# A hybrid decoder trunk: gate and up products of the FFN from seven blocks in place of eight, down projection in two rounds

## What is computed

```python
def rmsnorm(x, g):
    xf = x.astype(jnp.float32)
    y = xf * lax.rsqrt(jnp.mean(xf * xf, axis=-1, keepdims=True) + NORM_EPS)
    return (y * g.astype(jnp.float32)).astype(x.dtype)

def swiglu(h, w_gate, w_up, w_down):
    return (jax.nn.silu(h @ w_gate) * (h @ w_up)) @ w_down
...
        xp = xp + swiglu(rmsnorm(xp, norm_ffn[i]), ffn_w_gate[i], ffn_w_up[i], ffn_w_down[i])
        xs = xs + swiglu(rmsnorm(xs, norm_ffn[i]), ffn_w_gate[i], ffn_w_up[i], ffn_w_down[i])
```

## Time and profile before

| | |
|---|---|
| median of the runs | 2143.99 us (2139.22 to 2148.89, 3 runs) |
| the profiled execution | 2140.05 us |
| its span, first to last instruction | 2138.3 us |
| mean granted clock of TensorE | 0.996 of full |
| products of TensorE | 17508 |

### The profile page before, as it was taken

One profiled execution on the slowest core, in us unless ns is written; L12 is line 12 of the kernel. 1 busy time (PEld: TensorE's weight loads), 2 busy tenths in 40 slices (PEclk: granted clock), 3 DMA queues, 4 the chain that ended last, 5 costly groups with the idle time before them and its releaser, 6 DMA issues.

```text
span 2138.3 us, 42249 instructions
## 1 busy us (share of the span) xinstructions
PE 2095.1 (98%) x17508; PEld 2026.4 (95%) x17508; DVE 1004.1 (47%) x1374; ACT 912.0 (43%) x1218; POOL 263.6 (12%) x253
## 2 busy tenths in 40 slices
PE   8999999999899999999999979999999999999999
PEld 7999999997499999999999859999999989999999
DVE  6444433368764444333566646444442264444322
ACT  6434432265454344322677744434432263443221
POOL 4000001169320000001111122000001120000000
PEclk9999999999999999999999999999999999999999
DMA  5333333244223333332532433333323313333332
GB/s 186 94 93 93 88 91 92 67 126 118 58 80 89 93 93 88 91 92 78 174 119 81 141 126 99 89 88 89 98 84 89 110 51 94 97 88 89 96 103 59
DMA packets 349435, 207.24 MB, mean 97 GB/s; under 512 B 9385, under 2 KB 340041, under 8 KB 349300
## 3 DMA queue, kind: packets, MB, share of 16 engines
q1 hardware_dynamic: 345476, 198.26, 31.4%
q0 software_dynamic: 3472, 6.96, 1.0%
q10 hardware_dynamic: 384, 0.55, 0.1%
HBM read 194.53 MB, written 8.60 MB: 95 GB/s over the span
## 4 chain that ended last, share of the span: by engine, by line
PE 89%; POOL 4%; ACT 3%; DVE 3%; issue 1%; DMA 0%; SPq 0%; POOLq 0%; ACTq 0%; DVEq 0%
PE acc L564 82%; POOL conv L2149 4%; PE pair L929 1%; PE bank L949 1%; PE pair L904 1%; PE pair L645 1%; DVE pair L1776 1%; ACT w_hi L1160 1%; PE pair L1098 0%; ACT s_buf L1430 0%; DVE w_lo L1573 0%; PE bank L939 0%; PE acc L984 0%; PE acc L973 0%; PE acc L799 0%
## 5 line engine op out<-in xcount | busy, mean ns | idle before, releaser
L564 PE MATMUL acc<-xin_hi,w_hi 128*128 128x260 f32 x3456 | 982.5, 284 | 5.9 <-DVE w_lo L1573 4.7
L564 PE MATMUL acc<-xin_hi,w_lo 128*128 128x260 f32 x3456 | 976.5, 283 | 0.0
L564 PE MATMUL acc<-xin_lo,w_hi 128*128 128x260 f32 x3456 | 973.6, 282 | 0.0
L1160 ACT ACTIVATE w_hi<-raw 128x1024 fp32r<-128x1024 f32 (+1 forms) x332 | 344.9, 1039 | 972.8 <-PE acc L564 970.0
L564 PEld LDWEIGHTS acc<-xin_hi,w_hi 128*128 128x128 f32 x3456 | 650.4, 188 | 20.4 <-issue 13.9
L564 PEld LDWEIGHTS acc<-xin_lo,w_hi 128*128 128x128 f32 x3456 | 650.0, 188 | 0.2
L564 PEld LDWEIGHTS acc<-xin_hi,w_lo 128*128 128x128 f32 x3456 | 650.1, 188 | 0.0
L1573 DVE TENSOR_TENSOR w_lo<-raw,w_hi 128x1024 fp32r<-128x1024 f32 (+1 forms) x332 | 411.0, 1238 | 350.2 <-ACT w_hi L1160 350.1
L564 PE MATMUL acc<-h_hi,w_hi 128*128 128x260 f32 x1408 | 398.4, 283 | 0.0
L564 PE MATMUL acc<-h_lo,w_hi 128*128 128x260 f32 x1408 | 398.2, 283 | 0.0
L564 PE MATMUL acc<-h_hi,w_lo 128*128 128x260 f32 x1408 | 397.6, 282 | 0.0
(11 more groups left out here) (356 smaller groups left out, 1846.5 us busy)
## 6 DMA issues: line engine op xcount, KB each, us to landing
raw<-in_ffn_w_gate SPq DMA_DIRECT2D x88, 512.0 KB, 3.9
raw<-in_ffn_w_up SPq DMA_DIRECT2D x88, 512.0 KB, 3.9
raw<-in_ffn_w_down SPq DMA_DIRECT2D x64, 512.0 KB, 4.0
raw<-in_ffn_w_down SPq DMA_DIRECT2D x32, 384.0 KB, 3.5
raw<-in_attn_w_qkv SPq DMA_DIRECT2D x24, 512.0 KB, 3.9
raw<-in_conv_w_in SPq DMA_DIRECT2D x16, 512.0 KB, 4.0
raw<-in_conv_w_out SPq DMA_DIRECT2D x8, 512.0 KB, 4.3
in_mix<-in_cache_k SPq DMA_DIRECT2D x8, 512.0 KB, 5.0
```

What stands on the lines that cost most here:

```text
L564: last = pe.matmul(acc[:, b, 0:HALF], w[:, w_tile * P:(w_tile + 1) * P], v[:, h * HALF:(h + 1) * HALF], start=start and t == 0, stop=stop ...
L1160: act.activation(w_hi[n.slot(2)][:, 0:cols], raw[:, n.slot(4), 0:cols], ACT.Copy).then_inc(split_hi, 1)
```

## The change

Of the 22 pairs of a layer, four stay as they were ("plain", PLAIN = 4). For the other 18 the sum over the 1024 input channels is cut in two halves of 512, and the 520 tokens in two halves of 260. Gate and up tile are the two rows, the halves of the input channels the inner dimension, the halves of the tokens the columns of a product of 2x2 blocks. It is made from seven block products (of 4 weight tiles, 3 terms each) in place of eight, with sums and differences of blocks before and after:

- GpSimd makes four sums of weight blocks for each pair (w_sum, 512 columns each); it waits for both loads, and for low splits of the pair before (`sums`: behind that pair's fifth split for the first three, behind its last for the fourth).
- x is multiplied by gain and rstd once (xn0, xn1 by VectorE, 16 operations of 260 columns), GpSimd makes four differences of 1040 columns (xt, xt3), ScalarE and VectorE split seven blocks of x of 1040 columns (`x_high`, `x_low`).
- Weight blocks are split by the block, 512 columns, into a ring of seven (w_hi, w_lo and ring_hi, ring_lo); `high` and `low` of the next pair stand between the steps that `join` this one.
- Seven banks take one block each. ScalarE copies the first out; VectorE makes five sums from the banks, 260 or 520 columns each (`join`), then h2 = up2*silu2 and h_lo. The silu is made in halves of 260 columns, without a multiplication by rstd.
- TensorE waits before a pair's first block for the fourth of the five sums of the pair before (joined), which frees the two banks of pair.
- h_hi and h_lo hold 11 tiles, not 22. So a layer is: 4 plain and 7 block pairs, the down products of these 11 tiles (8 output tiles, units of 6 and 5 weight tiles), 11 block pairs, the down products of those. x is updated in both rounds. SyncE, ScalarE and VectorE follow this order.

The core of the diff. The buffers, banks and names of semaphores are left out, and the parts that only carry the new names of units.

```diff
+PLAIN = 4
+ROUND = (PLAIN + 7, 11)
+FH = 11
+PAIRS = FT - PLAIN
+FIRST_PAIR = (0, ROUND[0] - PLAIN)
...
+        X_SUMMED = (0, 0, 2, 4, 1, 3, 0)
+        X_READ = (1, 3, 3, 4, 2, 3, 0)
+        BLOCK_BANK = tuple(acc[:, b, 0:HALF] for b in (0, 2, 1, 3)) + (pair[:, 1, 0:HALF], pair[:, 0, 0:HALF], bank6[:, 0:HALF])
+        W_SUM = (None, None, 1, 2, 0, None, 3)
...
+                for half in range(2):
+                    first_j, last_j = FIRST_PAIR[half], (FIRST_PAIR[1], PAIRS)[half]
+                    for j in range(first_j, last_j):
+                        for g in range(2):
+                            if j < first_j + 2:
+                                sp.wait_ge(split_lo, base + DOWN[half] - 4 + 2 * (j - first_j) + g + 1)
+                            else:
+                                sp.wait_ge(blk_lo, 7 * (PAIRS * layer + j - 1))
+                            into_raw((raw_of_pair(layer, j) + g) % 4, gate_up(g, PLAIN + j), 1024)
...
+                def block(J, b, x_from):
+                    pe.wait_ge(blk_lo, (J.times(7) + (b + 1)).v)
+                    if x_from:
+                        pe.wait_ge(xs_lo_ok, 7 * layer + b + 1)
+                    to = BLOCK_BANK[b]
+                    hi, lo = ring(w_hi, ring_hi, b), ring(w_lo, ring_lo, b)
+                    _, x_hi, x_lo = XS[b]
+                    for k in range(4):
+                        cols = slice(k * P, (k + 1) * P)
+                        for t, (w, v) in enumerate(((hi, x_hi), (hi, x_lo), (lo, x_hi))):
+                            last = pe.matmul(to, w[:, cols], v[:, k, :], start=k + t == 0, stop=k == 3 and t == 2)
+                    last.then_inc(blk_done, 1)
+                def seven_blocks(J, half=None):
+                    x_from = half == 0
+                    if half is not None:
+                        pe.wait_ge(evacuated, m0 + DOWN_M[half] - 1)
+                    if J.i is not None or J.start:
+                        pe.wait_ge(first_ok, J.v)
+                        pe.wait_ge(joined, (J.times(5) + -1).v)
+                    block(J, 0, x_from)
+                    if half is not None:
+                        pe.wait_ge(evacuated, m0 + DOWN_M[half])
+                    for b in range(1, 6):
+                        block(J, b, x_from)
+                    if J.i is not None or J.start:
+                        pe.wait_ge(joined, J.times(5).v)
+                    block(J, 6, x_from)
+                def down(half, i):
                     for c in range(4):
-                        m = at(m0 + 2 * FT + c, 4, i)
-                        for j, (k0, k1) in enumerate(((0, 8), (8, 16), (16, FT))):
+                        d, m = at(u + DOWN[half] + 2 * c, 8, i), at(m0 + DOWN_M[half] + c, 4, i)
+                        for j, (k0, k1) in enumerate(((0, 6), (6, FH))):
                             def before(k):
-                                pe.wait_ge(h_lo_ok, FT * layer + k + 1)
-                            unit(at(u + 2 * FT + 3 * c + j, 12, i), m, h_hi, h_lo, k0, k1, FT,
-                                 before if c == 0 else None)
-                            if layer >= 2 and j == 0 and i + c:
+                                pe.wait_ge(h_lo_ok, FT * layer + FH * half + k + 1)
+                            unit(d + j, m, h_hi, h_lo, k0, k1, FH, before if c == 0 else None)
...
+                def x_high(b):
+                    act.wait_ge(x_scaled, layer + 1)
+                    if X_SUMMED[b]:
+                        act.wait_ge(x_summed, 4 * layer + X_SUMMED[b])
+                    own, hi, _ = XS[b]
+                    act.activation(hi, own, ACT.Copy).then_inc(xs_hi_ok, 1)
...
+                def high(J, q, b):
+                    if b < 2:
+                        act.wait_ge(landed[q.slot(4)], (q.turn(4).v + 1) * 16)
+                    elif b == 5:
+                        act.wait_ge(landed[(q + 1).slot(4)], ((q + 1).turn(4).v + 1) * 16)
+                    else:
+                        act.wait_ge(w_summed, (J.times(4) + (W_SUM[b] + 1)).v)
+                    act.activation(ring(w_hi, ring_hi, b), block_of(b, q), ACT.Copy).then_inc(blk_hi, 1)
+                def join(p, fh, nxt):
+                    for b in range(7):
+                        act.wait_ge(blk_done, (p.times(7) + (b + 1)).v)
+                        if b == 0:
+                            act.activation(first[:], acc[:, 0, 0:HALF], ACT.Copy).then_inc(first_ok, 1)
+                        if b == 4:
+                            act.wait_ge(joined, (p.times(5) + 1).v)
+                            act.activation(silu2[:, 0:HALF], silu2[:, 0:HALF], ACT.Silu).then_inc(gate0_ok, 1)
+                        if b < 6:
+                            nxt(b)
+                    f = fh + FT * layer
+                    act.wait_ge(joined, (p.times(5) + 5).v)
+                    act.activation(silu2[:, HALF:T], silu2[:, HALF:T], ACT.Silu).then_inc(sg_ready, 1)
+                    nxt(6)
+                    act.wait_ge(h_ready, (f + 1).v)
+                    act.activation(tile_of(h_hi, fh + -FH * (fh.start >= FH)), h2[:], ACT.Copy).then_inc(h_hi_ok, 1)
...
+                    for b in range(7):
+                        act.wait_ge(units_done, units - (b < 2))
+                        high(At(J0), At(q0), b)
+                        if half == 0 and b in (3, 4):
+                            x_high(b + 2)
+                    with act.Fori(0, (count - 1) // 2) as i:
+                        for c in range(2):
+                            def nxt(b):
+                                high(At(J0 + 1 + c, 2, i), At(q0 + 2 + 2 * c, 4, i), b)
+                            join(At(J0 + c, 2, i), At(f0 + c, 2, i), nxt)
...
+                def scaled(k):
+                    g = vec[:, V_FFN + 8 * layer + k:V_FFN + 8 * layer + k + 1]
+                    for h, to in enumerate((xn0, xn1)):
+                        cols = slice(h * HALF, (h + 1) * HALF)
+                        last = dve.scalar_tensor_tensor(to[:, k, :], x[:, k, cols], g, rstd[:, cols], ALU.mult, ALU.mult)
+                    return last
...
+                    dve.tensor_tensor(h2[:], up2[:], silu2, ALU.mult).then_inc(h_ready, 1)
+                    if c + 1 < PLAIN:
                         split(n + 3)
-                        dve.wait_ge(h_hi_ok, (f + (FT * layer + 1)).v)
-                        dve.tensor_tensor(tile_of(h_lo, f), h_buf[:, c, :], tile_of(h_hi, f).bitcast(F32), ALU.subtract)\
-                           .then_inc(h_lo_ok, 1)
+                    dve.wait_ge(h_hi_ok, f + 1)
+                    dve.tensor_tensor(h_lo[:, c, :], h2[:], h_hi[:, c, :].bitcast(F32), ALU.subtract).then_inc(h_lo_ok, 1)
+                    if c == 0:
+                        for k in range(4, KT):
+                            last = scaled(k)
+                        last.then_inc(x_scaled, 1)
+                    for b in ((), (0,), (1, 2, 3), (4,))[c]:
+                        x_low(b)
...
+                def low(J, q, b):
+                    dve.wait_ge(blk_hi, (J.times(7) + (b + 1)).v)
+                    dve.tensor_tensor(ring(w_lo, ring_lo, b), block_of(b, q), ring(w_hi, ring_hi, b).bitcast(F32), ALU.subtract)\
+                       .then_inc(blk_lo, 1)
+                def join(p, fh, nxt):
+                    done, made = p.times(7), p.times(5)
+                    dve.wait_ge(blk_done, (done + 1).v)
+                    nxt(0)
+                    dve.wait_ge(blk_done, (done + 2).v)
+                    nxt(1)
+                    dve.wait_ge(blk_done, (done + 3).v)
+                    dve.wait_ge(first_ok, (p + 1).v)
+                    dve.tensor_tensor(begun[:, 0:2, :], acc[:, 1:3, 0:HALF], first[:].unsqueeze(1).to_broadcast([P, 2, HALF]), ALU.add)                       .then_inc(joined, 1)
+                    nxt(2)
+                    dve.wait_ge(blk_done, (done + 4).v)
+                    dve.wait_ge(joined, (made + 1).v)
+                    dve.tensor_tensor(with_t3[:], acc[:, 3, 0:HALF], with_t2, ALU.add).then_inc(joined, 1)
+                    nxt(3)
+                    dve.wait_ge(blk_done, (done + 5).v)
+                    dve.tensor_tensor(with_t1[:], BLOCK_BANK[4], with_t2, ALU.add).then_inc(joined, 1)
+                    nxt(4)
+                    dve.wait_ge(blk_done, (done + 6).v)
+                    dve.wait_ge(joined, (made + 2).v)
+                    dve.tensor_tensor(halves(up2[:]), pair[:, :, 0:HALF], with_t3[:].unsqueeze(1).to_broadcast([P, 2, HALF]), ALU.add)                       .then_inc(joined, 1)
+                    nxt(5)
+                    dve.wait_ge(blk_done, (done + 7).v)
+                    dve.wait_ge(joined, (made + 3).v)
+                    dve.tensor_tensor(silu2[:, HALF:T], BLOCK_BANK[6], with_t1[:], ALU.add).then_inc(joined, 1)
+                    f = fh + FT * layer
+                    dve.wait_ge(sg_ready, (f + 1).v)
+                    dve.wait_ge(joined, (made + 5).v)
```

(45 more changed lines are left out.)

308 lines of the change are left out of this document (218 added, 90 removed).

## The result

| | before | after |
|---|---|---|
| median of the runs, us | 2141.66 (2139.22 to 2148.89) | 2170.78 (2168.77 to 2175.86) |
| profiled execution, us (span) | 2140.05 (2138.3) | 2175.86 (2173.9) |
| TensorE busy, us (products) | 2095.1 (17508) | 2034.7 (16644) |

A forecast was written before the change was run, and what follows sets the result against it. TensorE bounds the old kernel; in the changed pair loops VectorE, held up by GpSimd's sums, would at 11.3 us a pair. 2140 + 22 (layers) + 2 (rest) = 2164; with the median 3.9 higher, 2168, range 2112 to 2208.

The forecast's parts named there:

- TensorE's share: Block pairs on TensorE: 84 products in place of 96, 10.06 us against 11.50; 103.5 us saved at most.
- rival A: Pair loops: TensorE stays the bound as GpSimd's sums miss VectorE's splits; pair 10.06 us, median 2077; chance 0.12.
- VectorE alone, 8.87 us: VectorE's operations and waits in a pair, without GpSimd's interference, sum to 8.87 us, less than TensorE's 10.06.
- The door: SBUF access shared by GpSimd and VectorE: an addition costs VectorE 1.0 us when its next instruction reads SBUF twice.
- The layout: Pair's instructions laid out from the fifth split's end: GpSimd's sums delay VectorE, giving a period of 11.3 us.
- The start of a round: TensorE waits 5.4 us before a layer's first block pair, 1.6 before the eighth; first bank release after 15.0 and 12.1.
- A layer: A layer's 18 block pairs gain 1.4 us and pay 7.0 for the starts: +5.6, +22 in four layers.
- Table loads: ScalarE's table loads, 11 a layer, should leave the pair loops; if they stay, its idle 4 us a pair hide them.
- Loads of weights: Both loads of a pair land 10.9 us after issue, just before GpSimd's sums need them; no cost counted.
- rival D: TensorE's pauses lower its clock to 1.2 GHz in places; 3.4 us at half pace eat 1.2; chance 0.19 with rival C.
- The sum: Whole kernel: 2140 + 22 + 2 = 2164 us for the profiled execution; median forecast 2168.
- rival C: Pair loops: GpSimd holds 1.30 us or late loads make three sums block fully; period 11.8 to 12.1; 0.19 with rival D.

The follow-up runs named there:

- the probe with 8 columns: Changed kernel with GpSimd's four sums a pair cut to 8 columns of constants, splits of those blocks taking raw weights: 2079.83 us, ratio 0.9691.
- second order: Changed kernel with splits and PSUM sums reordered, third PSUM sum behind the fifth split, GpSimd's fourth sum released by its pair's second split: 2127.89 us, ratio 0.9933.
- third order: Kernel of the second order with the sixth and seventh split moved behind h_lo, so five splits follow in a row: 2132.3 us, ratio 0.9949.

## Why the prediction was right, step by step

- **TensorE's share.** 10.06 us a pair and 103.5 us at most: the last pair of a round, which follows no backlog, came 9.8 after the one before it, and without GpSimd's holds the time was 2079.8 (rival A's 2077). That rival's mechanism was right and only its condition wasn't met.
- **VectorE alone, 8.87 us.** Its operations have the predicted prices (0.69, 0.42; 0.58 idle for the silu, of the 0.67 laid out); alone they are no bound, as the probe with 8 columns shows.
- **The door.** An addition was to cost 1.0 when the next operation reads SBUF twice; it cost 1.1 (1.78 for 0.69). By the Trainium skill (GPSIMD Engine Reference, Elementwise — side-by-side cycle accounting) an fp32 addition with two inputs goes at some 2.6 cycles an element at 1.2 GHz; 512 elements would be 1.11 us, an estimate that agrees with the hold better than the record of 1.27 does. The layout put the holds on the sixth split (0.6), the seventh and the next pair's first (1.07 each): the trace has 0.68, 1.1 and 1.1, in just these places. The period laid out was 11.3; it is 11.30 to 11.34 in 47 of the 56 pairs, 11.5 at the head of each second round, and 11.5 to 11.9 in five single pairs.
- **The start of a round.** 5.4 and 1.6 were predicted, 5.3 and 1.5 are there. The way from the first split to the first release, 15.0 and 12.1 in the forecast, is 14.4 to 14.7 and 12.4, but that is luck, as its parts don't hold: none of the seven splits was held in these first pairs. GpSimd's first sum was kept out instead (below), its third and fourth came late, and VectorE waited 2.6 us for the high half of a sum. Round one took 81.7 us from the end of its first split to the first down product, as predicted, round two 125.0 for 124.0.
- **A layer.** Forecast +5.6 and 0.5 for the rest; measured +8.1, +7.6, +7.0 and +8.2 by the spans above. Five late pairs and the four heads of second rounds, 2.8 us together, are 0.7 of the 1.6 that are missing in the mean layer; I haven't found the rest in one place.
- **Table loads** left the pair loops: four are left where the silu of the plain tiles starts. **Loads of weights** are in time in 51 of the 56 pairs; the other five stand behind this list.
- **The clock** (rival D) stays at 1.00 in the steady pairs with TensorE busy 91% of the time (47.17 of 51.90 us, 126.5 to 178.4), as expected. It falls to 0.50 once in each round. In the first rounds that is at the start, where TensorE is ahead, as the forecast had it. In the second rounds it is for 3.4 us behind the 2.3 us that TensorE waits for the first `up`; this makes the 11.5 at their head, 0.2 us each, as rival D has it for a fall in mid-round. Where it cost most, before layer 0, no step of mine had looked.
- **The sum**: +24 for the profiled execution; its layers took +30.8, so the mechanism was right and the terms a little small (6.1 a layer for 7.7). Medians moved +29.1 against +24; that the forecast's 2168 stands only 2.8 below the median is partly luck, as the median before is now 2141.66 and no longer the 2143.99 from which it was worked out.

In five pairs GpSimd's first sum began 0.2 to 1.2 us late. In four of them the profile puts it down to the load of the up tile; in the fifth it names a split that had long been done, so there too it was probably a load:

```profile
726.92 1.72 POOL L2445 TENSOR_TENSOR w_sum<-raw 128x512 f32<-128x512 f32 x1 [4.88 <-DMA raw<-in_ffn_w_up]
```

In four of the five the sixth split goes free and three full holds follow, on the seventh, h_lo and the next pair's first, and the period is 11.7 to 11.9. That is what rival C describes. The forecast let the loads land 0.4 us before the sum needs them and counted nothing for them; they cost 2.0 us in all.

The experiments also show what the prediction treated too simply. I wrote as if the pauses at the starts were a cost of their own, 7.0 a layer. Taken away in the changed kernel they gave some 7 of 27 us, in the second order nothing, in the third 8.5. There are two reasons. While another engine is behind, a pause of TensorE is time in which that engine catches up: of the 27 us only 10 to 14 reach the first release of the rounds. And in the second and third order the fall of the granted clock behind the wait that is left takes another 11 to 14.

## What to carry to other kernels

Before work goes from the bound engine to an idle one, lay out both helpers' instructions in time, and price each of GpSimd's two-input SBUF operations of 512 columns at 1.1 us of VectorE wherever VectorE's next instruction reads SBUF twice; here 288 of them cost 86 us and turned 0.9691 of the time before into 1.0096. Then order the helpers so that GpSimd works while VectorE reads PSUM or waits: the same arithmetic in another order, with the earlier starts, gave 0.9902 of the time before in place of 1.0132. A pause of the bound engine is worth its length only once the engine behind it has no backlog, and where the wait only moves to another place, look at the granted clock behind it.
